# A two-layer transformer and a state-space block: the z chunks issued in pairs

## The reference, cut to what matters

```python
y_f = ssd_chunked(xh, dt_f, a_f, bm, cm)
y_b = flip(ssd_chunked(flip(xh), flip(dt_b), a_b, flip(bm), flip(cm)))
y = y_f + y_b + d_skip[:, None] * xh
y = y.reshape(bsz, s, D_INNER) * jax.nn.silu(z)
yg = y.reshape(bsz, s, SSD_GROUPS, D_INNER // SSD_GROUPS)
yg = yg * lax.rsqrt(mean(square(yg), -1) + NORM_EPS)
```

## Time and profile before

| | us |
|---|---|
| time, median of 3 | 1807.45 (1804.89 to 1808.73) |
| time of the profiled execution | 1812.81 |
| its span | 1811.0 |
| PE busy | 1564.4 |
| DVE busy | 755.5 |
| ACT busy | 566.8 |
| the 16 steps | about 1358 to 1480 us of the span |

### The profile page before, as it was taken

How to read it: one execution, slowest core, us unless ns; L and a number is a source line. 1 busy time by engine, 2 the same in 40 slices (tenths; PEclk the granted TensorE clock), 3 DMA queues, 4 the chain that set the end, 5 groups by cost and what they waited for, 6 DMA issues and landing times. The chain is left out here.

```text
span 1811.0 us, 20902 instructions
## 1 busy us (share of the span) xinstructions
PE 1564.4 (86%) x8780; PEld 1188.8 (66%) x8780; DVE 755.5 (42%) x1071; ACT 566.8 (31%) x850; POOL 50.9 (3%) x61
## 2 busy tenths in 40 slices
PE   6998959888869889986989886989987979879896
PEld 6986754343348778874434334978886869779785
DVE  3645440111145445423101014348767864455444
ACT  3344311000012244321100011347656664235331
POOL 0000000000000000000000001000011200000000
PEclk9999869999989955576999997979988989889998
DMA  7543338999953400012999995332231124435351
GB/s 293 189 176 140 108 123 361 419 426 422 422 202 140 155 32 0 1 47 87 399 411 406 427 422 224 140 140 93 95 138 47 48 94 156 151 136 186 140 190 66
DMA packets 25664, 355.45 MB, mean 196 GB/s; under 512 B 2848, under 2 KB 2848, under 8 KB 3552
## 3 DMA queue, kind: packets, MB, share of 16 engines
q1 hardware_dynamic: 23760, 341.85, 47.8%
q0 software_dynamic: 1808, 12.22, 1.7%
HBM read 353.01 MB, written 1.05 MB: 196 GB/s over the span
## 5 line engine op out<-in xcount | busy, mean ns | idle before, releaser
L1609 DVE TENSOR_TENSOR ring_low<-ring,w_rounded 128x2048 fp32r<-128x2048 f32 (+1 forms) x128 | 291.1, 2275 | 363.8 <-ACT w_rounded L1230 363.7
L1230 ACT ACTIVATE w_rounded<-ring 128x2048 fp32r<-128x2048 f32 (+1 forms) x128 | 242.9, 1900 | 390.0 <-PE ps L701 139.8
L687 PE MATMUL ps<-split,w_rounded 128*128 128x256 f32 x1056 | 259.5, 296 | 32.1 <-DVE ring_low L1609 21.2
L823 PE MATMUL ps<-ring,work 128*64 128x512 f32 x1024 | 234.3, 607 | 23.0 <-DMA ring<-slabs 19.4
L687 PE MATMUL ps<-split,ring_low 128*128 128x256 f32 x800 | 236.0, 295 | 0.0
L687 PEld LDWEIGHTS ps<-split,w_rounded 128*128 128x128 f32 x1056 | 194.4, 202 | 38.0 <-issue 28.8
L823 PEld LDWEIGHTS ps<-ring,work 128*64 128x64 f32 x1024 | 73.2, 139 | 163.8 <-issue 140.4
L701 PE MATMUL ps<-w_rounded,split 128*128 128x512 f32 (+1 forms) x448 | 156.9, 402 | 11.9 <-DVE split L2232 7.0
L687 PEld LDWEIGHTS ps<-split,ring_low 128*128 128x128 f32 x800 | 162.5, 203 | 0.0
L687 PE MATMUL ps<-hT_low,w_rounded 128*128 128x256 f32 x544 | 162.3, 298 | 0.0
L854 PE MATMUL ps<-ring,work 128*64 128x512 f32 x512 | 118.3, 606 | 31.8 <-DMA ring<-slabs 31.8
(11 more groups left out here) (313 smaller groups left out, 2188.0 us busy)
## 6 DMA issues: line engine op xcount, KB each, us to landing
ring<-slabs SPq DMA_DIRECT2D x162, 2048.0 KB, 9.0
gb<-ln_gb POOLq DMA_DIRECT2D x6, 1024.0 KB, 5.0
hT<-x_feat SPq DMA_DIRECT2D x1, 1024.0 KB, 5.0
work<-c_ret POOLq DMA_DIRECT2D x1, 1024.0 KB, 12.1
h<-x_tok POOLq DMA_DIRECT2D x1, 1024.0 KB, 22.0
y<-w_pattn POOLq DMA_DIRECT2D x1, 1024.0 KB, 7.7
out<-h SPq DMA_DIRECT2D x2, 512.0 KB, 2.6
work<-c_nsa POOLq DMA_DIRECT2D x1, 944.0 KB, 6.7
```

Source lines behind the costliest of these rows:

```text
L687: last = nc.tensor.matmul(dst[:, at:at + T], w3[a][:, k, c * P:(c + 1) * P], src[b][:, k, :], start=(k == 0 and t == 0), stop=(k == KC - 1 ...
L823: last = nc.tensor.matmul(bank(b)[e * CAP:(e + 1) * CAP, :], m_xT[:, e2 % 2, 4 * half + k, e * CAP:(e + 1) * CAP], w4[:, e, k, :], start=( ...
L1230: nc.scalar.activation(rounded_half(q), half_of(ring, q), ACT.Copy).then_inc(w_high, 1)
L1609: V.tensor_tensor(half_of(ring_low, q), half_of(ring, q), rounded_half(q).bitcast(F32), ALU.subtract).then_inc(w_low, 1)
```

## The change

The call of z_chunk moves under a condition: in steps with even c two chunks are issued, in the others none.

```diff
@@ for p in range(16): g, c = divmod(p, 4)
                 if p < 15:
                     decay_rows(2 * p + 2)
                     decay_rows(2 * p + 3)
-                z_chunk(p)
+                if c % 2 == 0:
+                    z_chunk(p)
+                    z_chunk(p + 1)
                 if c == 1 and g < 3:
```

## The result

| | before | after |
|---|---|---|
| time, median of 5 | 1807.45 us (1804.89 to 1809.30) | 1821.41 us (1816.61 to 1826.73) |
| ratio, 95% interval | | 1.0075 [1.0048, 1.0101] |
| time of the profiled execution | 1812.81 us | 1826.73 us |
| its span | 1811.0 us | 1825.0 us |
| stretch from chunk 4 to the gates | 90.12 us | 96.84 us |

The account below looks back on a forecast made before the run. The prediction took the PE, ScalarE and VectorE loop of each group, not DMA, as the bound. 4.1 + 3.6 + 3.2 - 2.15 = 8.7 us, taken as 7.4, on 1807.45 gave 1814.8 us (+0.4%), range 1810.0 to 1819.0.

Parts of the forecast that it names:

- The loop: Each group is one chain: SiLU, first z chunk, diagonals, decay rows, clamp, exp, next SiLU; PE work there delays everything.
- ScalarE's 2.15 us: Weight rounding at the end of group 3 waits 2.15 us for chunk 15; the change removes that wait.
- C: Rival: group 0 is late too, chunks 2 and 3 meeting the low clock; 2 us more, 1816.8 us; chance 0.12.
- A: Rival: longer bursts keep PE's clock up at chunks 4, 8 and 12; about -1 us, 1806.5 us; chance 0.06.
- B: Rival: the delay is hidden and only the 2.15 us gain at the end shows, 1805.3 us; chance 0.06.
- group 1: Steps 4 to 7: first clamp 3.3 us late behind chunks 4 and 5, 4.1 us late in all by step 7.
- group 2: From chunk 8: first clamp 3.2 us late behind the pair, second half adding 0.4 us.
- group 3: From chunk 12: first clamp 3.2 us late behind the pair.
- the end: End of group 3: chunk 15 comes before the diagonals of step 14, giving 2.15 us back.
- the low stretch of a pair: After PE's idle time ahead of a group's first pair, the lower clock lasts 7.3 us; in group 2 the pair takes 9.1 us.
- one low stretch per group: The clock is low only at a group's first pair; work behind the odd-step wait was priced at the upper clock.
- short low stretches: Allowance for low stretches shorter than 7.3 us: a mean of 6.3 us, 3 x 0.44 us off the 8.7 us sum.

Follow-up runs that it names:

- e2: Kernel after, but only the first half of each group issues paired z chunks: ratio 1.0042, stretch from chunk 4 to the gates 94.48 us.
- e5: Kernel after, but only the second half of each group issues paired z chunks: ratio 1.0015, stretch 89.71 us.
- e4: Kernel after, but only group 0 (chunks 0 to 3) is paired: ratio 0.9988, stretch 88.50 us.
- e8: Kernel before, unchanged, run again as a control: ratio 1.0005, stretch 88.19 us.
- e1: Kernel after, unchanged, run again beside before: ratio 1.0063, median 1821.63 us, stretch 96.49 us.
- e9: Kernel after, with the last transpose of x repeated 11 times in PE's wait in steps 5 and 9: ratio 1.0044, stretch 95.65 us.
- e10: Kernel after, with both PE's waits for the z SiLU and its odd-step waits filled by repeated work: ratio 1.0016, stretch 89.93 us.
- e6: Kernel after, with the last decay-row matmul ahead of a pair repeated 40 times in PE's wait for the SiLU: ratio 1.0045, stretch 95.04 us.
- e12: Kernel before, with chunk 15 in step 14, step 15's diagonals issued twice and filler matmuls in four PE waits behind the heads: 1802.52 us, ratio 0.9969.

## Why the prediction was right in kind and wrong in time

- **The loop was right.** Decay rows queue behind the second chunk, VectorE's waits for them went from one to three with 7.4 us (I had said some 8), PE idles longer ahead of chunk 8 (5.45 us), ScalarE's 2.15 us are gone, and PE meets the exp of the odd step. e2 and e5 show that the pair in front of a group's first decay rows costs more than the other (5.6 against 3.3 us). e4 excludes C; A and B are excluded by clamps 9.5 us behind their restart and by loops of 34.3 us from SiLU to SiLU (30.5 and 31.0 before).
- **Terms.** In the first profiles of before and after, with the forecast in brackets: group 1 +1.8 (+3.3) and +2.0 (+0.75); group 2 +1.7 (+3.2) and +1.6 (+0.4); group 3 +1.6 (+3.2); the end -2.0 (-2.15). Sum 6.7 us (8.7, taken as 7.4).
- **First step that failed: the low stretch of a pair.** "With 5.5 us idle I take the low stretch as 7.3 us" was too much; it was 3.6 to 4.0 us behind idle times of 5.45 and 7.12 us, and the pair took 7.6 us, not 9.1. I had assumed that a longer idle time makes it no shorter, from two rows of 5.40 and 4.93 us. The runs don't bear that out: in the kernel before chunk 4 was faster after 6.61 us idle (e8) than after 5.40, and with 3.74 and 3.75 us idle chunk 8 took 4.38 and 5.29 us. Nothing on record says ahead of a run how long the low stretch will be. In after and e1 all six were short, 3.4 to 4.0 us; behind the same 5.45 us idle e9 has 4.6 and 5.1.
- **Second step that failed: one low stretch per group.** I saw PE's new wait in the odd step ("It meets another wait instead") and then priced all that follows it at the upper clock. That let me put the second half of a group at +0.75 and +0.4 us. The clock fell there too, and it was +2.0 and +1.6 us. e10 against e6 shows it: only when that wait is filled as well do the 6.7 us come back. At the upper clock my price was nearly right: e10 needs 15.5 us from the first clamp of a group to that of c = 3, where I had worked out 15.25. The first error made the sum 4.6 us too large, the second 2.5 us too small, and I had taken off 1.3 us for short low stretches. That 7.4 came so close to 6.7 is luck.
- **Third step: where the sum was set down.** I added 7.4 us to 1807.45, the median of three executions, and let the range end at 11.5 us above it. The kernel before had medians of 1811.07, 1810.09, 1811.72 and 1809.05 us beside the experiments, on average 3.0 us higher. Put down on 1811.07, beside which after ran again, the forecast is 1818.5 us and the range 1813.6 to 1822.6, against a measured 1821.63. So this term alone, 3 to 4 us, is enough to put the time outside. The range allowed for the change's unknowns and for nothing else.
- **What stays open.** The stretch explains 7.7 us of 10.6 to 14. Behind it the profiles of after have 326.83 and 326.69 us, those of before 326.14 and 325.75, but the experiments whose code there is the same cover 324.90 to 326.79 us, so the 0.8 us can't be laid on the change. For e1 the stretch alone is enough, its interval begins at 7.1 us. The first comparison begins at 8.7 us, 1 us above the stretch. Its profile of after lost some 5 us in the experts, ahead of the change, and e1 did not lose them. What else made up the 3 to 6 us is not shown.

The advice of the Trainium skill weighed in the prediction (TensorE: Matmul & The Clock Gate, HAM oscillation — how this bites in real kernels) is to do more of the matmuls ahead of the next wait, so that PE stays warm; the section gives it for thin matmuls that wait for DMA. Here all three pairs, twice as long as a chunk, still started at the lower clock, and a second low stretch appeared; what helped was work inside the wait (e10, e12), not behind it.

## What to carry to other kernels

Before work is bunched on the engine that others wait for, find the first small product behind the bunch that another engine needs: here four decay-row matmuls behind 24 more z matmuls made one wait of the stage into three, and the time that the bunch frees later lands in a wait. When a forecast says that PE will newly wait somewhere, price what follows at the lower clock too, and treat all the waits of a loop together: filling one of two gained 1 to 2 us, both 6.7. And set the sum on a base whose own spread is in the range; three executions are a thin one.

## What the runs showed of the hardware

- How long the clock stayed low after a restart doesn't follow from the idle time before it. By the last slow start of a matmul: about 7.3 us after 5.40 us idle and 3.1 after 3.74, over 5 after 3.75 (e8), 3.8 after 6.61 (e8), 4.0 after 7.12 (after), 3.6 to 3.8 after 5.45 (after), 4.6 and 5.1 after 5.45 (e9).
- The clock could also fall behind a wait of only 1.2 us and sixteen matmuls of 2 columns: the next diagonals took 2.3 to 2.8 us instead of 1.52 (after, e1, e6, step 9 of e2). It did not always, step 5 of e2 has the same wait and 1.52 us. Without the wait, with repeated transposes in its place, steps 5 and 9 took 1.52 us (e9, e10).
- Filling one wait moved the low clock to another place: in e6 from the pair to the odd step (square sums 3.09 us), in e9 from the odd step to the pairs (up to 8.1 us). Each is one profile, and low stretches vary that much by themselves; what both fillings give together (e10) doesn't hang on it.
- Useless matmuls in waits paid: 81 of them, 128x128, with the diagonals doubled, are the whole of e12 beside chunk 15 moved. The mean clock of an execution rose from 0.890 to 0.897 (medians over the executions of before and of e12).
